# Where xT and the stage buffers start in SBUF: two padding buffers of a two-block transformer kernel made 64 and 32 bytes longer

## The reference

```python
def swiglu(x, w_gate, w_up, w_down):
    return (jax.nn.silu(x @ w_gate) * (x @ w_up)) @ w_down

x = layer_norm(alpha * x + 0.5 * swiglu(x, ffn_w_gate[l, 0], ffn_w_up[l, 0], ffn_w_down[l, 0]), ...)
x = layer_norm(alpha * x + hybrid_mixer(x, w_in[l], ...), ...)
x = layer_norm(alpha * x + 0.5 * swiglu(x, ffn_w_gate[l, 1], ffn_w_up[l, 1], ffn_w_down[l, 1]), ...)
...
u = rmsnorm(h, norm_mix_pre[i]);  ya = gdn_mixer(...);  yb = nsa_mixer(...)
h = h + rmsnorm((g_a * (ya @ w_a2d[i]) + g_b * (yb @ w_b2d[i])) @ w_o[i], norm_mix_post[i])
f = causal_dwconv(rmsnorm(h, norm_ffn_pre[i]) @ w_up[i], conv_ffn[i]) + conv_ffn_b[i]
h = h + rmsnorm((gelu(f_gate) * f_val) @ w_down[i], norm_ffn_post[i])
e = (p[i] @ w_ple[i]) * sigmoid(h @ w_ple_gate[i]);  h = h + rmsnorm(e, norm_ple_post[i])
```

## The kernel before, in words

| buffer | before, modulo 1024 | after, modulo 1024 |
|---|---|---|
| ring, weights_high, weights_low (a block: + 512 each) | 128 | 128 |
| cst (identity and masks) | 128 | 128 |
| xs, res | 736 | 736 |
| xT_high, xT_low | 64 | 128 |
| stat | 64 | 128 |
| tmp | 384 | 448 |
| hT, hf, act_buf, gel, mT, oT, yT, rcs, pE, v1, cv, gates1 | 32 | 128 |
| xc, rc | 288 | 384 |
| gates2, ot0 | 896 | 992 |

## Time and profile before

### The profile page before, as it was taken

The page is one execution under the profiler, slowest core; times in us unless marked ns, Lnnn a source line. Parts: engine busy times, 40 slices in busy tenths (PEclk is TensorE's granted clock), DMA queues, the critical chain, the costliest instruction groups (busy, mean ns, idle before and its releaser), DMA issues.

```text
span 1116.0 us, 22283 instructions
## 1 busy us (share of the span) xinstructions
PE 1093.5 (98%) x8110; PEld 1024.4 (92%) x8110; DVE 498.3 (45%) x904; ACT 620.9 (56%) x1002; POOL 897.0 (80%) x695
## 2 busy tenths in 40 slices
PE   8999999999999999999999999999999999999996
PEld 8999998999998998999999899999999798999985
DVE  4422113201456564431125663884765356545563
ACT  4444444644666765544444686655766565555564
POOL 6999996897664586999999599676355798999985
PEclk9999999999999999999999999999999999999999
DMA  7866665675342454766665466445134565666652
GB/s 243 279 202 202 188 192 173 196 240 187 114 133 76 133 168 135 229 205 191 193 196 173 133 188 193 148 132 152 61 99 136 177 201 170 190 188 190 194 181 76
DMA packets 52774, 191.29 MB, mean 171 GB/s; under 512 B 5856, under 2 KB 6112, under 8 KB 52320
## 3 DMA queue, kind: packets, MB, share of 16 engines
q1 hardware_dynamic: 50688, 182.47, 52.0%
q10 hardware_dynamic: 2016, 7.81, 2.1%
HBM read 189.21 MB, written 1.05 MB: 170 GB/s over the span
## 4 chain that ended last, share of the span: by engine, by line
POOL 55%; issue 28%; PE 14%; POOLq 1%; ACT 1%; DMA 1%; DVE 0%; SPq 0%; DVEq 0%; ACTq 0%
POOL weights_low L537 55%; PE banks L579 8%; PE acc L579 6%; DMA ring<-in_stream 1%; POOLq L543 0%; POOLq L534 0%; ACT tmp L1699 0%; ACT tmp L1969 0%; ACT weights_high L1451 0%; DVE res L2175 0%; POOL stat L551 0%; POOLq L314 0%; PE banks L688 0%; DVE xs L2187 0%; SPq L498 0%
## 5 line engine op out<-in xcount | busy, mean ns | idle before, releaser
L537 POOL TENSOR_TENSOR weights_low<-ring,weights_high 128x512 fp32r<-128x512 f32 x686 | 893.9, 1335 | 207.0 <-ACT weights_high L1451 204.9
L1451 ACT CAST weights_high<-ring 128x1024 fp32r<-128x1024 f32 x343 | 356.1, 1048 | 214.0 <-PE banks L579 124.9
L579 PE MATMUL banks<-xT_high,weights_high 128*128 128x256 f32 x1264 | 351.0, 278 | 1.1 <-POOL weights_low L537 1.1
L579 PE MATMUL banks<-xT_low,weights_high 128*128 128x256 f32 x1264 | 349.8, 277 | 0.0
L579 PE MATMUL banks<-xT_high,weights_low 128*128 128x256 f32 x1264 | 349.8, 277 | 0.0
L579 PEld LDWEIGHTS banks<-xT_high,weights_high 128*128 128x128 f32 x1264 | 237.4, 188 | 4.3 <-issue 1.5
L579 PEld LDWEIGHTS banks<-xT_low,weights_high 128*128 128x128 f32 x1264 | 237.6, 188 | 2.2
L579 PEld LDWEIGHTS banks<-xT_high,weights_low 128*128 128x128 f32 x1264 | 237.5, 188 | 0.0
L2004 DVE TENSOR_TENSOR hf<-act_buf,banks 128x256 f32<-128x256 f32 x40 | 16.9, 421 | 225.0 <-ACT act_buf L1477 210.9
L579 PE MATMUL acc<-xT_high,weights_high 128*128 128x256 f32 x408 | 109.7, 289 | 1.5 <-ACT xT_high L1552 1.0
L579 PE MATMUL acc<-weights_high,hT_high 128*128 128x512 f32 x264 | 104.2, 395 | 1.5 <-POOL weights_low L537 1.5
(11 more groups left out here) (363 smaller groups left out, 1579.6 us busy)
## 6 DMA issues: line engine op xcount, KB each, us to landing
ring<-in_stream SPq DMA_DIRECT2D x343, 512.0 KB, 3.6
rows<-in_big_rows ACTq DMA_DIRECT2D x3, 1024.0 KB, 5.6
rows<-in_big_rows ACTq DMA_DIRECT2D x3, 512.0 KB, 4.6
cst<-in_consts ACTq DMA_DIRECT2D x3, 470.5 KB, 4.9
xs<-in_x_tm ACTq DMA_DIRECT2D x2, 512.0 KB, 7.2
out<-xs SPq DMA_DIRECT2D x4, 256.0 KB, 2.1
gates<-in_x_fm SPq DMA_DIRECT2D x2, 256.0 KB, 4.2
ring<-in_stream SPq DMA_DIRECT2D x2, 256.0 KB, 3.9
```

Source lines behind the costliest of these rows:

```text
L537: last = nc.gpsimd.tensor_tensor(wlo[:, slot, hs], ring[:, slot, hs], whi[:, slot, hs].bitcast(F32), ALU.subtract)
L579: ins = nc.tensor.matmul(o, lhsT, rhs, start=start, stop=stop, **kw)
L1451: nc.scalar.copy(whi[:, ch % RING, :], ring[:, ch % RING, :]).then_inc(S["hi_ready"], 1)
```

## The change

Nobody's padding `fill_x` grows from 88 to 104 floats, `fill_stage` from 144 to 152. That moves xT, stat, tmp and the small buffers behind them by 64 bytes, and every stage buffer by 96 bytes. Nothing else differs: each engine has the same instructions with the same waits in the same order. Stationary and moving operands of all the matmuls with weights then begin at 128 modulo 512.

```diff
@@ -334,7 +334,7 @@
         srow = sb("srow", [N_SROW])
         xs = sb("xs", [2, 2, D])
         res = sb("res", [2, D])
-        sb("fill_x", [88])
+        sb("fill_x", [104])
         xT = pair("xT", [KD, T])
         stat = sb("stat", [64])
         sb("fill_scalars", [12])
@@ -343,7 +343,7 @@
         nmx2 = sb("nmx2", [2, 4])
         den2 = sb("den2", [2, 4])
         coef2 = sb("coef2", [2, 4])
-        sb("fill_stage", [144])
+        sb("fill_stage", [152])
         hT = pair("hT", [GROUP, T], in_ffn)
         hf = sb("hf", [2, T], in_ffn)
         act_buf = sb("act_buf", [2, 2 * T], in_ffn)
```

## The result

| | before | after |
|---|---|---|
| median of the runs, us | 1119.11 (1118.62 to 1119.55) | 1139.09 (1138.66 to 1139.43) |
| profiled execution, us | 1117.81 | 1139.07 |
| its span, us | 1116.0 | 1137.3 |

The account below looks back on a forecast made before the run. PE was taken to bound the kernel, by matmul count times pitch. Gains of 4.0, 1.0 and 2.0 us made -7.0, so 1117.8 became 1110.8, plus 1.0 for the median 1111.8, say 1112 us; range 1108 to 1137.

Parts of the forecast that it names:

- What bounds the kernel: Whole kernel: PE is busy 1093.5 of 1116.0 us, so time is the number of matmuls times their pitch.
- (1): Down projections, hT from 32 to 128: 792 matmuls falling from 233.3 to 228.2 ns, 4.0 us gained.
- (2): Output projections of the two mixers, mT from 32 to 128: 192 matmuls at 233.3 ns, 1.0 us gained.
- (3): Branch projections, moving oT and yT from 32 to 128: pitch from 118.8 and 120 towards 113.3 ns, 2.0 us gained.
- (4): Projections with xT moving, from 64 to 128: 5016 matmuls staying at 113.3 ns, zero change taken; 21 us lost at worst.
- (5): POOL, ACT and DVE beside PE: POOL can follow a faster PE; zero taken, with 1 us to either side.
- the first, both operands at the same place: All matmuls with weights: load and stream ask for the same memory part, one waits; 1133 to 1138 us, chance 0.35.
- The second rival: All the matmuls: place matters not or little, or a small xT loss eats the gain; 1116.6 to 1121, chance 0.15.
- The third rival: xT matmuls: operands at the same boundary avoid the excess over 106.7 ns; about 1090 us, chance 0.04.

Follow-up runs that it names:

- e1: Kernel before with only the stage buffers moved, from 32 to 128 modulo 1024, xT left at 64: 1122.7 us, ratio 1.0030.
- e2: Kernel before with only xT moved, from 64 to 128, stage buffers left at 32 modulo 1024: 1141.93 us, ratio 1.0200.
- e3: Against the kernel before: xT and stage buffers at 128 as in the changed kernel, weights, cst, xs and res 64 bytes further: 1116.89 us, ratio 0.9979.
- e4: The changed kernel with every buffer 64 bytes further, ring and weights included: 1138.79 us, ratio 1.0176.
- m1: Separate program replacing the whole computation, TensorE alone, mapping operand distances through 512 bytes by 32: 113.3 to 120.0 ns for 256 columns.
- e5: Kernel before with the stage buffers moved to 64, xT staying at 64: median 1119.49 us, executions 1115.3 to 1123.2, ratio 0.9999.
- e9: The kernel of e5 unchanged, profiled a second time, on a different chip: 1118.57 us for that execution.

## Why the prediction was wrong

The forecast was 1112 us with a range of 1108 to 1137; 1139.1 is outside, on the other side of no change. By its steps:

- **What bounds the kernel**: right. PE's pitch by place of the two operands was the thing to read, and all that changed.
- **(1), (2) hT and mT**: right in size, and by luck. 4.0 and 1.0 us were forecast, 4.9 and 0.7 came, and e1 shows that they are their own (181.1 and 44.5 us there too). But the reason given, a loaded operand at a multiple of 64, isn't it: in the map the distances 64 and 128 leave 512 columns at 233.3 and 232.4 ns, and only 0 and -64 gain. The change happened to go to 0.
- **(3) oT and yT**: wrong for the same reason as (4), 2.0 us forecast, 0.3 lost. They went from 118 to 120 ns and not to 113.3.
- **(4) xT**: the step that failed. It took zero, on the ground that 64 and 128 are both multiples of 64. Measured: 5016 steps from 114.2 to 119.8 ns, 28 us by the means and 26 by the sums. e2 has it alone, e3 takes it away with xT at the same 128, e4 keeps it with everything elsewhere. So what counts is the distance between the two operands modulo 256, and only -64 has the low pitch for 256 columns. The alignment to 64 bytes, on which (1) to (4) were sorted, is not a property that counts: in m1 the distance 64 has 117.8 ns and 128 has 119 to 120, and both are multiples of 64 as well.
- **(5) the other engines**: right. POOL's 892.1 against 893.9 us, more idle time. VectorE's `hT_low` got shorter, 1003 to 720 ns on the mean, under PE as before.

Of the rivals, the first, both operands at the same place, gave the right direction and nearly the size. What it named right is that the load beside the stream matters, and the two operands' places relative to each other. Its reason, that one waits where both ask for the same part of the memory, isn't borne out: at distance 0 streams of 512 columns have their lowest pitch, 226.7 ns, and for 256 columns the distance 96 is as slow as 0. Its price was too low as well. It took the 117.9 ns of the earlier trace rows for the bad state, 1133 to 1138; the pitch at distance 0 is 120.0. The 117.9 ns was another state of the old distance. The yT rows with 120 ns would have been the better bound from above: the largest pitch of this shape in the trace. The second rival (place doesn't matter) fell with e2 and e3. It is also what the Trainium skill gives ("SBUF — State Buffer", "Who interferes with whom", and "TensorE: Matmul & The Clock Gate", "Back-to-back issue gap"): two independent read ports, and a gap of N / 2.4 + 2.5 ns, 109.2 ns for 256 columns, with no term for the place. That section gives the formula for a matmul by itself and says that it leaves out the weight loads of a real stream, which the prediction passed over. The runs differ: m1, with TensorE alone and a load for each matmul, has 113.3 ns at the best of places and 120.0 at the worst, and the measurement decides. The third rival, 106.7 ns, was met at none of the 16 distances.

What misled the sorting was that the steady stretches of these shapes in the trace of before hold only two distances, -64 and -96. Two explanations fitted them, the distance and the alignment of one operand, and they disagree exactly about the change. Nothing in the trace favoured the alignment, so the 0.35 for the rival should not have been the smaller chance.

Open: why -64 is favourable for 256 columns and 128 loaded ones, and why it has two states. With 64 loaded columns the order of the distances is turned round (113.3 ns at 0, 119.2 at -64), and the period is 256 bytes; the runs don't show what in the memory has that period. What picks the state at the start of a layer wasn't found either. It differs between executions of one program, so it is not in the program alone.

## What to carry to other kernels

Where a matmul's stream and the next weight load take about the same time (here 256 columns of fp32r against 128 loaded ones), its pitch depends on the distance between the two operands in SBUF modulo 256 bytes; the best distance is another one for another number of columns (-64 for 256, 0 for 512), so it has to be measured for the shape that does most of the work. Here that was 6% of a pitch, and TensorE was busy all the time either way, so only the pitch shows it. Take pitches from the timeline over stretches of dozens of matmuls and sort them by the places of both operands, and before moving a buffer run a map of all distances with TensorE alone: this one took 300 us of chip time and had the result of the change in it. A placement whose steady stretch has two states is a gamble for each execution; it needs many executions before its median means anything.

## What was not expected of the hardware

- Two lasting states at one placement, 113.3 and 117.8 ns, the second handed on from the stretch before, or differing between two executions (e5 and e9, the same program, on two chips): 3.6 us per feed-forward layer.
- For up to 240 columns the fp32r matmul with a new 128-column load has a pitch of 111 to 112 ns, whatever its columns and at each of the three distances tried. Below 240 columns, fewer columns save nothing.
- VectorE's subtraction with two operands in SBUF (`hT_low`) took 1003 ns before and 720 ns after, with the same operands of 256 columns. It isn't their place: e2, with hT where it was before, has 693 ns, and e3, with hT where it is after, 1023. It goes with the length of the tile. In the third feed-forward layer the mean is 602 to 603 ns where its tiles take 8.5 us or more (after, e2, e4), 953 to 988 at 8.4 us (e1, e5, e9) and 1139 to 1283 at 8.2 to 8.3 us (the others), where GpSimd idles least. Why it does wasn't tested.
